# High parts first in every first quad of a two-block transformer kernel, later RWKV output weights, and one weight slot rounded sooner

## What is computed

```python
def first_block(x, ...):                      # two layers
    mix = merged(conv, diff_attention, nsa_attention of x @ w_in) @ w_o
    x = layer_norm(ALPHA * x + mix)
    h = causal_dwconv(x @ w_up) + conv_b      # conv FFN
    x = layer_norm(ALPHA * x + (gelu(a) * u) @ w_down)

def second_block(x, mem, ...):                # layer 0: RG-LRU, layer 1: RWKV-7
    x = x + rms_norm(mixer(rms_norm(x)))      # each mixer ends in an output GEMM w_out / w_o
    x = x + rms_norm(mem_cross_attention(rms_norm(x), mem_n, w_q, w_kv, w_o))
    x = x + rms_norm(square(relu(rms_norm(x) @ w_up)) @ w_down)
```

## Time and profile before

| | us |
|---|---|
| median of 3 runs | 3537.31 (3535.99 to 3541.93) |
| the profiled execution, own time | 3544.32 |
| its span from the first to the last instruction | 3542.5 |
| mean granted TensorE clock, share of full speed | 0.996 |
| TensorE matmul busy | 3478.3, 19096 instructions |
| VectorE / ScalarE / GpSimd busy | 1689.1 / 1355.1 / 1259.8 |
| DMA moved | 313.17 MB, mean 88 GB/s |

### The profile page before, as it was taken

How to read it: one execution, slowest core, us unless ns; L and a number is a source line. 1 busy time by engine, 2 the same in 40 slices (tenths; PEclk the granted TensorE clock), 3 DMA queues, 4 the chain that set the end, 5 groups by cost and what they waited for, 6 DMA issues and landing times.

```text
span 3542.5 us, 51209 instructions
## 1 busy us (share of the span) xinstructions
PE 3478.3 (98%) x19096; PEld 2692.5 (76%) x19096; DVE 1689.1 (48%) x2640; ACT 1355.1 (38%) x2310; POOL 1259.8 (36%) x601
## 2 busy tenths in 40 slices
PE   9999999999999999999999999999999999999998
PEld 7877787888788777878887677788864477768886
DVE  2655657442334665754324743513245875435041
ACT  3345524332323454333325644423314244444232
POOL 4422244444444222434443143344400022424443
PEclk9999999999999999999999999999999999999999
DMA  4421122223234111222232322222232311213322
GB/s 147 125 78 53 54 80 94 96 95 101 95 106 125 48 56 64 95 89 95 97 105 95 101 101 70 86 95 95 98 107 77 88 39 56 95 54 102 101 95 83
DMA packets 103380, 313.17 MB, mean 88 GB/s; under 512 B 26912, under 2 KB 29088, under 8 KB 102560
## 3 DMA queue, kind: packets, MB, share of 16 engines
q1 hardware_dynamic: 88160, 299.42, 25.3%
q10 hardware_dynamic: 15040, 11.23, 1.3%
HBM read 302.23 MB, written 5.24 MB: 87 GB/s over the span
## 4 chain that ended last, share of the span: by engine, by line
issue 44%; PE 35%; POOL 17%; DVE 2%; DMA 1%; DVEq 1%; POOLq 0%; SPq 0%; ACT 0%; ACTq 0%
POOL ring_r L2966 17%; PE ps L551 9%; PE ps L553 9%; PE ps L552 9%; PE ps L1174 1%; DMA ring<-in_weights 1%; PE ps L928 1%; PE ps L1103 1%; DVE Z L2829 1%; PE ps L1129 1%; DVE SOLVE_TMP L2826 1%; PE ps L1280 0%; SPq L522 0%; PE ps L1272 0%; PE ps L1324 0%
## 5 line engine op out<-in xcount | busy, mean ns | idle before, releaser
L2966 POOL TENSOR_TENSOR ring_r<-ring,rounded_r 128x1024 fp32r<-128x1024 f32 x499 | 1221.0, 2449 | 1919.5 <-ACT rounded_r L1437 1910.9
L551 PE MATMUL ps<-source_hi,rounded_r 128*128 128x512 f32 x2560 | 1020.5, 399 | 24.2 <-POOL ring_r L2966 6.4
L1437 ACT ACTIVATE rounded_r<-ring 128x1024 fp32r<-128x1024 f32 x504 | 533.8, 1059 | 1333.5 <-PE ps L553 1203.9
L552 PE MATMUL ps<-source_hi,ring_r 128*128 128x512 f32 x2560 | 998.4, 390 | 0.0
L553 PE MATMUL ps<-X_lo,rounded_r 128*128 128x512 f32 x1536 | 600.2, 391 | 0.0
L551 PEld LDWEIGHTS ps<-source_hi,rounded_r 128*128 128x128 f32 x2560 | 481.6, 188 | 154.3 <-issue 20.9
L552 PEld LDWEIGHTS ps<-source_hi,ring_r 128*128 128x128 f32 x2560 | 481.9, 188 | 95.7 <-issue 2.4
L553 PEld LDWEIGHTS ps<-X_lo,rounded_r 128*128 128x128 f32 x1536 | 289.0, 188 | 61.8
L553 PE MATMUL ps<-N_lo,rounded_r 128*128 128x512 f32 x768 | 299.3, 390 | 0.0
L2486 DVE SCALAR_TENSOR_TENSOR T<-ps,PAR,T 128x511 f32<-128x511 f32 (+1 forms) x176 | 131.5, 749 | 227.2 <-ACT T L1680 211.0
L551 PE MATMUL ps<-H_hi,rounded_r 128*128 128x512 f32 x512 | 199.2, 389 | 0.0
(11 more groups left out here) (498 smaller groups left out, 5060.8 us busy)
## 6 DMA issues: line engine op xcount, KB each, us to landing
ring<-in_weights SPq DMA_DIRECT2D x556, 512.0 KB, 3.3
X<-in_x SPq DMA_DIRECT2D x4, 512.0 KB, 6.9
PAIR<-Z ACTq DMA_DIRECT2D x32, 64.0 KB
ring<-in_weights SPq DMA_DIRECT2D x16, 128.0 KB, 2.6
out_x<-X SPq DMA_DIRECT2D x4, 512.0 KB, 2.7
SWAP<-Z ACTq DMA_DIRECT2D x4, 256.0 KB, 6.2
MEM<-in_mem ACTq DMA_DIRECT2D x1, 1024.0 KB, 4.7
mem_keys<-Z ACTq DMA_DIRECT2D x1, 1024.0 KB, 4.2
```

What stands on the lines that cost most here:

```text
L551: mm(o, lh, rh, start=start, stop=False)
L552: mm(o, ll, rh, start=False, stop=False)
L1437: av(RH[:, j, :], ring[:, j, :], ACT.Copy).then_inc(w_hi, 1)
L2966: nc.gpsimd.tensor_tensor(RL[:, j, :], ring[:, j, :], RH[:, j, :].bitcast(F32), ALU.subtract).then_inc(w_lo, 1)
```

## The change

The change does three things.

`first_quad` becomes `high_first`, at all 15 calls. For each tile k it takes the two matmuls with the source's high part for all lanes, after a wait on the high part's semaphore, and then the low matmul of tile k - 1 for all lanes, after a wait on the low part's. The last tile's low matmuls of all lanes stand at the end. The skewed form has the same idea for its first three tiles. The number of matmuls and their operands stay the same; only their order, and the waits, differ.

In both tails the slot 3 of the MLP's first quad is rounded inside `split_in`, before tile 5, and not after it; its remainder is taken by VectorE between `residual` and `in_squares`, and GpSimd's loop leaves it out.

The pieces of RWKV's output weights are issued when `rw["tok"]` is 6 and not 2, and U_WO is 8 and not 3.

```diff
-U_WO = 3
+U_WO = 8
...
-            sp.wait_ge(rw["tok"], 2)
+            sp.wait_ge(rw["tok"], 6)
...
-            def first_quad(split, bank, hi, lo, ready, base, step=1, banks_free=None, lanes=RING - 1, before=None, skewed=False, late=None):
-
-                def step_of(k, j):
-                    pe.wait_ge(ready, base + step * (k + 1))
+            def high_first(split, bank, hi, lo, rounded, at, ready, base, step=1, banks_free=None, lanes=RING - 1, before=None, skewed=False, late=None):
+
+                def high(k, j):
+                    pe.wait_ge(rounded, at + k + 1)
                     if k == 0:
                         if j == 2 and late is not None:
                             late()
                         pe.wait_ge(w_lo, split + (j + 1))
                         if banks_free is not None:
                             pe.wait_ge(banks_free[0], banks_free[1] + (j + 1))
-                    ins = three(ps[:, bank + j, :], wh(j, k), wl(j, k), tile(hi, k), tile(lo, k), k == 0, k == KT - 1)
+                    mm(ps[:, bank + j, :], wh(j, k), tile(hi, k), start=k == 0, stop=False)
+                    mm(ps[:, bank + j, :], wl(j, k), tile(hi, k), start=False, stop=False)
+
+                def low(k, j):
+                    pe.wait_ge(ready, base + step * (k + 1))
+                    ins = mm(ps[:, bank + j, :], wh(j, k), tile(lo, k), start=False, stop=k == KT - 1)
                     if k == KT - 1:
                         ins.then_inc(used, 1)
 
                 if skewed:
                     for j in range(2):
-                        for k in range(2):
-                            step_of(k, j)
+                        high(0, j)
+                        high(1, j)
+                        low(0, j)
                     for j in range(2):
-                        step_of(2, j)
+                        high(2, j)
+                        low(1, j)
                     for k in range(3):
-                        step_of(k, 2)
-                for k in range(3 if skewed else 0, KT):
+                        high(k, 2)
+                    for k in range(2):
+                        low(k, 2)
+                for k in range(3 if skewed else 0, KT + 1):
                     if before is not None and k == before[0]:
                         before[1]()
-                    for j in range(lanes):
-                        step_of(k, j)
+                    if k < KT:
+                        for j in range(lanes):
+                            high(k, j)
+                    if k > 0:
+                        for j in range(lanes):
+                            low(k - 1, j)
...
-            def split_in(residual, gain, first=0, end=KT + 1):
+            def split_in(residual, gain, first=0, end=KT + 1, slot_at=None):
 
                 for n in range(first, end):
+                    if slot_at is not None and n == slot_at[1]:
+                        last_slot(slot_at[0])
...
-                split_in(2 + 3 * l, gain(l, 4))
-                last_slot((B + B_MFF) // RING)
+                split_in(2 + 3 * l, gain(l, 4), slot_at=((B + B_MFF) // RING, 5))
...
                 residual(4 + 6 * l, low_of(gain(l, 4), SRC[f"up{l}"]))
+                last = n_split(B + B_MFF) + RING - 1
+                dve.wait_ge(w_hi, last + 1)
+                dve.wait_ge(w_lo, last)
+                remainder(RL[:, RING - 1, :], ring[:, RING - 1, :], RH[:, RING - 1, :].bitcast(F32), w_lo)
                 in_squares(5 + 6 * l)
...
+            def but_last_slot(first, end, quad):
+
+                remainders(n_split(first), (quad - first) // RING)
+                for j in range(RING - 1):
+                    remainder(n_split(quad) + j, j)
+                pool.wait_ge(w_lo, n_split(quad) + RING)
+                remainders(n_split(quad) + RING, (end - quad) // RING - 1)
```

More of the change, by code:

```diff
@@ L741, in _ @@
                         mm(ps[:, 7, :], RS[:, 0:P], RS[:], start=True, stop=True)
-                first_quad(W0, 0, XH, XL, x_ready, l * 16, 2, (zc, l * C_Z), 1 if l == 0 else RING - 1)
+                rounded, at = (src_hi, 0) if l == 0 else (ln["hi"], KT)
+                high_first(W0, 0, XH, XL, rounded, at, x_ready, l * 16, 2, (zc, l * C_Z), 1 if l == 0 else RING - 1)
                 with pe.Fori(1, Z_DQ // RING) as i:
@@ L859, in _ @@
                             turn_diff()
-                first_quad(W0 + n_split(B_WO), 0, MR, ML, y_lo, l * Y_N + 12, 1, (mg, l * 24 + 24), skewed=True)
+                high_first(W0 + n_split(B_WO), 0, MR, ML, y_hi, l * Y_N + 12, y_lo, l * Y_N + 12, 1, (mg, l * 24 + 24), skewed=True)
                 shift(l, 0)
@@ L871, in _ @@
                 warm(7, 2)
-                first_quad(W0 + n_split(B_UP), 0, XH, XL, x1, l * KT, 1, (up_c, l * C_UP))
+                high_first(W0 + n_split(B_UP), 0, XH, XL, ln["hi"], l * 2 * KT, x1, l * KT, 1, (up_c, l * C_UP))
                 with pe.Fori(1, C_UP // RING) as i:
@@ L934, in gemm @@
                 if src is not None:
-                    first_quad(n_split(first), bank, hi, lo, src_lo, src, 1, (free, base), lanes, before, skewed, late)
+                    high_first(n_split(first), bank, hi, lo, src_hi, HI0 + src, src_lo, src, 1, (free, base), lanes, before, skewed, late)
                     done = 1
@@ L2985, in _ @@
                 remainders(W0 + n_split(B_MERGE), (CPL - B_MERGE) // RING)
-            for first, n in SPLIT_RUNS[:2]:
-                remainders(n_split(first), n // RING)
+            def but_last_slot(first, end, quad):
[4 more added lines that the diff above has]
+                remainders(n_split(quad) + RING, (end - quad) // RING - 1)
+            first, n = SPLIT_RUNS[0]
+            remainders(n_split(first), n // RING)
+            first, n = SPLIT_RUNS[1]
+            but_last_slot(first, first + n, B_TAIL0 + B_MFF)
             for n in range(KT):
@@ L3020, in _ @@
             remainder(n_split(first) + RING - 1, RING - 1)
-            remainders(n_split(first) + RING, n // RING - 1)
+            but_last_slot(first + RING, first + n, B_TAIL1 + B_MFF)
             for t in range(0, KT, 2):
```

## The result

| | us |
|---|---|
| before, median of 20 runs | 3538.85 (3535.99 to 3543.27) |
| after, median of 20 runs | 3544.03 (3542.03 to 3547.31) |
| ratio after / before | 1.0014, 95% interval 1.0008 to 1.002 |
| the profiled execution of after, own time / span | 3543.25 / 3541.4 |
| mean granted clock | 0.997 |

The change costs 5.2 us at the medians, 2.8 to 7.1 by the interval: slower, though by less than the 0.2% (7.1 us) that the prediction took as the line. The two profiled executions say the opposite (3541.4 against 3542.5). The profiled execution of before took 3544.32, above all 20 timed runs of before (highest 3543.27), so it was an unusual one; the medians decide.

A forecast was written before the change was run, and what follows sets the result against it. TensorE, busy 98%, was taken as bound at next quads by slot 0's release. Gains of 2.77 against losses of 6.75 gave +4.0, with the pieces +3.3, on 3537.31: 3540.6 us, main range 3537 to 3544, widened to 3531 to 3547.

The forecast's parts named there:

- What bounds the next quad: After each first quad: the next quad's start follows slot 0's release, which comes 0.91 us later against the lanes' end.
- UP, z, MLP up, RWKV out: First quads forecast to gain: UP twice and z of layer 1 1.35, MLP up 0.96, RWKV output 0.46 us.
- LRU in, LRU out, q, o: First quads forecast to lose: LRU in 0.68, LRU out 1.36, q projections 1.62, o projections 1.82 us.
- WO: WO's first quads: slot 0 freed 1.04 us later, slack absorbing part; 0.85 lost in layer 1, 0.42 in layer 0.
- Pieces: RWKV output weight pieces loaded in later units: 0.7 us gained, the slow clock coming back in one case of two.
- the pieces' stalls go: Rival, RWKV units: late units have no stalls, 4.6 us gained, total -0.6, 3536.7 us; chance 18%.
- the pieces meet more: Rival, RWKV units 5 to 10: early stalls stay and late pieces add 4.6 us, +8.6, 3546 us; chance 12%.
- The prediction's other reading: RWKV pieces: fetches share DMA engines with pieces wherever they stand, so stalls and slow clock follow; term 0, sum 3541.3 us.
- slot 0's chain gives way: Rival, next quads: slot 0's chain has slack and the lanes' ends count, 9.5 us gained with pieces, 3527.8; chance 15%.
- Slots land later: Rival, 14 places: slots freed closer together share DMA engines, +4 to +7 us on top, 3545 to 3548; chance 10%.

The follow-up runs named there:

- e7: Kernel before, only the last source tile of each three-lane first quad reordered, its low matmuls last (slot 0 freed 4 matmuls later): 3548.77 against 3538.59 us.
- e4: Changed kernel with lane 0's last low matmul in each first quad issued with 6 matmuls still to go: 3532.26 us against 3538.11 for the kernel before.
- e2: Kernel before with only the RWKV output weight pieces later (tok 6, U_WO 8): 3538.03 against 3538.11 us.
- e6: As e5, with 10 matmuls behind lane 0's last and 18 instead of 16 ahead of lane 2 at WO and LRU out: 3525.5 us against 3538.59 before.
- e5: As e4, with 8 matmuls behind lane 0's last instead of 6: 3528.92 us against 3538.59 for the kernel before.
- e8: e6 with the RWKV output weight pieces early, as before the change (tok 2, U_WO 3): 3527.31 us against 3539.21 for the kernel before.
- e9: e6 with e4's last tile at the two q projections: 3525.99 us against 3539.21 for the kernel before.
- e1: Changed kernel with only the new order of the first quads, output pieces and slot 3 as before: 3543.53 against 3538.11 us.

## Why the prediction was right

The forecast was +3.3 us and no difference above 0.2%; +5.2 was measured. The time, 3544.03, lies in the stated 3531 to 3547 and at the edge of the main range of 3537 to 3544; 1.5 us of the miss is the base, whose median was 3537.31 over 3 runs and is 3538.85 over 20.

- **What bounds the next quad**: slot 0's chain, as forecast. e7 shows the cost by itself and e4 takes it away; both were put in numbers beforehand (+10 and +10.2; -13 and -11.3 to -11.8). A page total of waits of "some 18 us" was forecast, 17.6 came.
- **UP, z, MLP up, RWKV out**: -2.77 forecast, -2.7 in the profile. The two MLP places differ (-0.11, -0.96) about their mean of 0.54, so that their sum came right by some luck: in the first the slot's DMA took 3.67 us from issue to landing, where it took 3.25 in before.
- **LRU in, LRU out, q, o**: 5.48 forecast, 5.15 measured. The o places paid 0.75, not 0.91, as the chain itself ran in 0.2 us less. It did so in e2 as well, with the old order (0.23 and 0.19 sooner), so the 0.2 lies in the profile of before; against e2 the o places paid 0.95 and 0.97.
- **WO, the term mis-sized**: 1.27 forecast, 2.74 measured. I had slot 0 freed 1.04 us later and a slack of 0.2 and 0.4 absorb part; for layer 0 that would even have left 0.64, not the 0.42 that went into the sum. Both halves were wrong. There is no slack: in before the remainder ends 0.14 us before TensorE's start at both WO places, the same 0.14 as at o, where TensorE waits, and e7 pays 0.91 and 0.81 there. And slot 0's DMA is issued 1.35 us later at both, because lane 2 waits for its PSUM bank, which VectorE's last gate frees (the wait on G_b, 0.4 us in before and 1.3 after). It starts at the same moment as before with two matmuls fewer done, and these come after it, as at LRU out:

```profile
523.16 0.47 PE L551 MATMUL ps<-M_hi,rounded_r 128*128 128x512 f32 x1 [0.19 <-DVE G_b L2470]
```

```profile
522.94 0.47 PE L582 MATMUL ps<-M_hi,rounded_r 128*128 128x512 f32 x1 [0.65 <-DVE G_b L2485]
```

(The first row is before, the second after.) Each place pays 0.45 + 0.91 = 1.36. The two parts show singly too: e4, with the release put back, pays 0.35 and 0.44, and e6, which puts back both, is 1.4 to 1.6 below after.
- **Pieces**: -0.7 forecast, -0.1 in e2's medians; not to be told apart. The forecast let the stall come back with the late pieces and gave the slow clock one chance in two. The profiles say otherwise: the stall is gone in all six with late pieces, and the slow clock stands in the profile of before alone. So "the pieces' stalls go" was right in kind, but worth some 1.6 us and not 4.6; "the pieces meet more" (+8.6) fell with e2. Taking a fallen clock from one execution as a property of the kernel was the weak step. The prediction's other reading, that the stalls come with the pieces wherever they stand, is not what these profiles show either.
- **The rival "slot 0's chain gives way" (3528)** was wrong for this kernel, and is what e4 to e6 turn it into: with the release out of the way, the lanes' ends do count (3528.92 in e5).
- **Slots land later**: not seen at 13 of the 14 places, where slot 0's DMA takes 3.13 to 3.40 us from issue to landing after the change and 3.13 to 3.44 before; the first MLP up is the exception (3.67).

WO's 1.5 and the pieces' 0.6, less 0.3 at LRU, q and o, make up the 1.9 us by which +3.3 missed; all but WO's term is within what the profiles and medians can tell.

## What to carry to other kernels

In a ring of buffers, a consumer that interleaves several slots decides by its last few instructions when the first slot is free; write that order from the release backwards, and let the work that releases nothing come last, as long as that chain still ends last (here 8 matmuls behind the release did in the profiles what 10 did). Removing a wait from the front of a stage is worth only what the next chain leaves; measure that chain from its release to its next use (at o 7.7 us against 7.0 of other work before, 7.5 against 6.1 after) before shortening what is ahead of it. And what one profile shows without a semaphore wants a second profile before it is put into a sum: here the stall recurred, the slow clock didn't.

## What the runs showed of the hardware

**A wait that moved into another engine's instruction.** In e4 z's next quad in layer 1 gained nothing although slot 0 was freed sooner. GpSimd's remainder of slot 0, which takes 2.40 us, showed 3.41 there. VectorE's last memset before it, then the remainder, then TensorE's start:

```profile
959.80 1.76 DVE L2336 MEMSET PAIR<- 128x2048 f32 x1 [0.38 <-issue]
...
960.54 3.41 POOL L2996 TENSOR_TENSOR ring_r<-ring,rounded_r 128x1024 fp32r<-128x1024 f32 x1 [20.62 <-ACT rounded_r L1462]
...
964.00 0.50 PE L551 MATMUL ps<-source_hi,rounded_r 128*128 128x512 f32 x1 [1.24 <-POOL ring_r L2996]
```

959.80 + 1.76 + 2.40 = 963.96, and 960.54 + 3.41 = 963.95: the remainder ran its full length after the memset's end. The same sum holds in e6, e8 and e9 (remainders of 2.90, 2.96 and 3.16 us beside the same memset), while in before, where it began after the memset, it is 2.40. The Trainium skill (SBUF — State Buffer, SBUF: two separate sides) says that VectorE and GpSimd share a port pair, that whichever starts first holds it for the whole instruction, and that the other fully blocks; for VectorE it names instructions in a 2-port mode or with two SBUF inputs. The full length after the memset's end agrees with the blocking. A memset has no SBUF input, and whether this one ran in such a mode no row shows.

**A stall alone didn't set the clock.** At LRU out TensorE stands 2.09 us on "issue" in e4 and 2.03 in after, at the same matmul. In e4 the clock then fell, the matmuls' pitch going from 0.23 to 0.43 us:

```profile
2031.27 0.47 PE L582 MATMUL ps<-source_hi,rounded_r 128*128 128x512 f32 x1 [2.09 <-issue]
...
2032.33 0.63 PE L582 MATMUL ps<-source_hi,rounded_r 128*128 128x512 f32 x1
2032.76 0.63 PE L583 MATMUL ps<-source_hi,ring_r 128*128 128x512 f32 x1
```

The granted clock of the 5 us that follow the stall, in e4 and in after:

```profile
2031.20:2036.20 5.00, 4.93 (x15) 0.66 0.00 0
```

```profile
2035.10:2040.10 5.00, 4.91 (x22) 1.00 0.00 0
```

15 matmuls against 22: the 1.2 GHz level for some of these 5 us cost LRU out 7 x 0.227 = 1.6 us in e4. With the 1.0 at z and the 0.8 at WO that is more than e4 fell short of; q and o made up the rest. The other runs divide as well: e5 has the same stall of 2.03 us and a fallen clock behind it (15 matmuls in 5 us, 0.66), e1 has it at 2.04 and keeps the full clock, and in the earlier trace rows the clock fell after a stall of 1.36 us that e1 and e8 show with the clock at 1.00. Why it falls in one and not in the other, no run here tells.
